# Scoring two attention heads together in the row halves of TensorE, with a new order of the work around it

## What is computed

```python
q, k = rms_norm(q, q_gain), rms_norm(k, k_gain)
logits = q @ k.T / 8 + bias[head, key] + mask[query, key]
p = softmax(logits)
o = p @ v
y = rms_norm(o by group of heads) * (a gate, for the forgetting heads)
x = x + y @ w_out
```

## Time and profile before

| | |
|---|---|
| median of 3 runs | 1564.51 us |
| the profiled execution | 1565.74 us, span 1563.9 us |
| PE matmul busy | 1496.9 us, 96% of the span |
| DVE busy, ACT busy | 844.1 us (54%), 616.3 us (39%) |
| granted TensorE clock, mean | 0.986 |
| chain that ended last | PE 85%, DVE 7%, POOL 4%, ACT 2% |
| the attention stage, in the trace | about 924 to 1180 us |

### The profile page before, as it was taken

One profiled execution on the slowest core, in us unless ns is written; L12 is line 12 of the kernel. 1 busy time (PEld: TensorE's weight loads), 2 busy tenths in 40 slices (PEclk: granted clock), 3 DMA queues, 4 the chain that ended last, 5 costly groups with the idle time before them and its releaser, 6 DMA issues.

```text
span 1563.9 us, 23462 instructions
## 1 busy us (share of the span) xinstructions
PE 1496.9 (96%) x9229; PEld 1290.1 (82%) x9229; DVE 844.1 (54%) x1227; ACT 616.3 (39%) x920; POOL 267.0 (17%) x272
## 2 busy tenths in 40 slices
PE   7978999999979999999997999999999999999998
PEld 7977999999968988988885777888886888888887
DVE  5779744357465543553455546776845533434344
ACT  5547655643243221231233334646534323223230
POOL 2664100000025613540632000000100000000000
PEclk9989999999999999999998999999999999999999
DMA  5211211123302222222232221111122222223221
GB/s 191 83 42 54 69 54 56 67 82 137 108 28 95 94 94 94 91 97 95 81 108 74 73 76 55 43 39 55 41 81 95 91 97 95 95 94 95 92 95 67
DMA packets 36006, 128.03 MB, mean 82 GB/s; under 512 B 4460, under 2 KB 4588, under 8 KB 35792
## 3 DMA queue, kind: packets, MB, share of 16 engines
q1 hardware_dynamic: 34464, 122.18, 23.3%
q10 hardware_dynamic: 864, 4.33, 0.7%
q0 software_dynamic: 592, 0.30, 0.1%
HBM read 124.68 MB, written 2.10 MB: 81 GB/s over the span
## 4 chain that ended last, share of the span: by engine, by line
PE 85%; DVE 7%; POOL 4%; ACT 2%; issue 2%; DMA 0%; SPq 0%; DVEq 0%; POOLq 0%; ACTq 0%
PE ps L1699 72%; PE ps L2036 2%; PE ps L2060 2%; PE ps L1881 1%; PE ps L1723 1%; POOL phase_tmp L1568 1%; PE ps L2047 1%; PE ps L1831 1%; DVE h_lo L866 1%; DVE w_lo L853 1%; PE ps L2014 1%; DVE x L866 1%; POOL acc L1568 1%; POOL phase L1568 1%; POOL conv_tmp L1657 1%
## 5 line engine op out<-in xcount | busy, mean ns | idle before, releaser
L1699 PE MATMUL ps<-h_hi,w_hi 128*128 128x258 f32 (+2 forms) x1768 | 512.3, 339 | 38.9 <-DVE h_lo L866 18.2
L1699 PE MATMUL ps<-h_lo,w_hi 128*128 128x258 f32 (+2 forms) x1768 | 494.3, 329 | 0.0
L1699 PE MATMUL ps<-h_hi,w_lo 128*128 128x258 f32 (+2 forms) x1768 | 493.2, 328 | 0.0
L853 DVE TENSOR_TENSOR w_lo<-w_raw,w_hi 128x1024 fp32r<-128x1024 f32 (+2 forms) x227 | 290.5, 1280 | 182.6 <-ACT w_hi L355 181.4
L1699 PEld LDWEIGHTS ps<-h_hi,w_hi 128*128 128x128 f32 x1768 | 301.9, 190 | 90.1 <-issue 34.8
L1699 PEld LDWEIGHTS ps<-h_lo,w_hi 128*128 128x128 f32 x1768 | 299.5, 190 | 33.8 <-issue 5.9
L1699 PEld LDWEIGHTS ps<-h_hi,w_lo 128*128 128x128 f32 x1768 | 299.5, 190 | 30.8
L355 ACT ACTIVATE w_hi<-w_raw 128x1024 fp32r<-128x1024 f32 (+2 forms) x227 | 233.2, 1035 | 199.6 <-PE ps L1699 198.6
L1699 PE MATMUL ps<-mlp_lo,w_hi 128*128 128x512 f32 x256 | 100.9, 394 | 0.0
L1699 PE MATMUL ps<-mlp_hi,w_hi 128*128 128x512 f32 x256 | 100.3, 392 | 0.0
L1699 PE MATMUL ps<-mlp_hi,w_lo 128*128 128x512 f32 x256 | 99.4, 388 | 0.0
(11 more groups left out here) (292 smaller groups left out, 1936.3 us busy)
## 6 DMA issues: line engine op xcount, KB each, us to landing
w_raw<-w_units SPq DMA_DIRECT2D x227, 512.0 KB, 3.3
x<-x_t ACTq DMA_DIRECT2D x1, 2112.0 KB, 7.8
out<-out_tile SPq DMA_DIRECT2D x8, 256.0 KB, 2.0
x<-x_t ACTq DMA_DIRECT2D x3, 528.0 KB, 9.2
x<-x_t ACTq DMA_DIRECT2D x2, 264.0 KB, 4.7
consts<-consts SPq DMA_DIRECT2D x1, 320.0 KB, 6.9
b_step<-ssm_b SPq DMA_DIRECT2D x1, 256.0 KB, 10.4
c_step<-ssm_c SPq DMA_DIRECT2D x1, 256.0 KB, 11.3
```

The costliest lines, as they stand in the source:

```text
L853: Dv.do(v.tensor_tensor(wlo[:, s % RING, 0:w], raw[:, s % RING, 0:w], f32(whi[:, s % RING, 0:w]), ALU.subtract), lo_ready)
L1699: ins = mm(o, wt[:, s % RING, w], xt[:, kx, c0:c0 + n], start=(b == 0 and a == 0), stop=(b == len(blocks) - 1 and a == 2))
```

## The change

1. Scores. q and k of a pair are kept as 128 rows (tiles q_pair, k_pair: head 0 in rows 0 to 63, head 1 in rows 64 to 127). One call scores both heads: first all masks of the pair, then for query tiles 1 and 3 the bias and the product of q and k, then the same for tiles 0 and 2. Bias and product of the two heads go to the two row halves of the array (`tile_position=(64 * hh, 0)`), each to its own PSUM bank. The bias is an fp32r matmul of its own: a selector (pair_sel_r) picks the head's row of key_bias_r, in which rows 0 to 15 hold the rounded bias and rows 32 to 47 the rest of it. The semaphore qk_mm is raised after each half.
2. Set-up. One DMA of 256 KB brings all linear biases, four small ones the forgetting heads' rows; 16 DMAs in the loop go away, and so do the two memsets of the ones (L1314). ACT gains two copies (pair_sel_r, key_bias_r), DVE two subtractions of 16x512, POOL three additions on 8 columns.
3. `qk_norm` ends in one operation of 128 rows for both heads, where it had two of 64 rows.
4. `maxima` and `exps` go by the query tiles 1, 3, 0, 2, and start on tile 1 when the first half of the scores is there.
5. Order. On PE both heads' transposes stand together after wide(i,1), and both heads' values after wide(i+1,0), followed by stat and the scores of the pair. On ACT a one-element exponential ahead of `exps` loads its table; both heads' exponentials follow each other. The tail is ordered in the same manner, and out_part(5) and (6) leave PSUM (DVE) after the dilated group's norm, where they stood before it.

```diff
-BANK_DONE = (3, 2, 3, 4)
+BANK_DONE = (4, 1, 4, 2)
+    T_ORDER = (1, 3, 0, 2)
...
             def maxima(i, hh):
-                dve.wait_ge(sem("qk_mm"), h + 1)
...
-                for t in range(4):
+                for t in T_ORDER:
+                    if t in (T_ORDER[0], T_ORDER[2]):
+                        dve.wait_ge(sem("qk_mm"), 2 * i + 1 + T_ORDER.index(t) // 2)
...
-            def scores(i, hh):
-                pe.wait_ge(sem("aug_ready"), 4 * i + 4)
-                pe.wait_ge(sem("qa_ones"), 2)
-                pe.wait_ge(sem(f"bias_in{i % 2}"), 32 * (i // 2 + 1))
-                if i:
-                    pe.wait_ge(sem("attn_done"), h - 1)
...
+            def scores(i):
+                pe.wait_ge(sem("aug_ready"), 2 * i + 2)
+                pe.wait_ge(sem("bias_lo"), 2)
...
+                rows_of = (slice(0, 64), slice(64, 128))
+                for t in T_ORDER:
...
+                    if t == 0 and i:
+                        pe.wait_ge(sem("attn_done"), 2 * i)
+                    for hh in range(2):
+                        if 2 * i + hh < N_MOBA + N_FOX:
+                            mm(PS[:, 2 + 3 * hh + bank, c + w - P:c + w], identr[:, :], maskr[:, :], start=(t != 2), stop=True,
...
+                for ts in (T_ORDER[:2], T_ORDER[2:]):
+                    for t in ts:
...
+                        for hh in range(2):
+                            mm(PS[:, 2 + 3 * hh + bank, c:c + w], selr[rows_of[hh], i, :], kbr[rows_of[hh], 0:w],
+                               start=False, stop=True, skip_group_check=True, tile_position=(64 * hh, 0))
+                    for t in ts:
...
+                        for hh in range(2):
+                            r = rows_of[hh]
+                            ins = mm(PS[:, 2 + 3 * hh + bank, c:c + w], qa[i % 2][r, P * t:P * t + P], ka[i % 2][r, 0:w],
+                                     start=False, stop=True, skip_group_check=True, tile_position=(64 * hh, 0))
+                    ins.then_inc(sem("qk_mm"), 1)
```

PE's loop:

```diff
                 if i >= 2:
-                    p_transposes(i - 2, 1)
+                    values(i - 2, 0)
...
                 qk_stat(i, 0)
+                scores(i - 1)
...
                 p_transposes(i - 1, 0)
-                scores(i - 1, 1)
-                values(i - 1, 0)
+                p_transposes(i - 1, 1)
                 qk_stat(i, 1)
```

PE's tail:

```diff
             out_part(0)
+            values(KT - 2, 0)
+            values(KT - 2, 1)
...
             out_part(1)
-            p_transposes(KT - 2, 1)
-            scores(KT - 1, 0)
-            values(KT - 2, 1)
+            scores(KT - 1)
             out_part(2)
             out_part(3)
             p_transposes(KT - 1, 0)
-            scores(KT - 1, 1)
+            p_transposes(KT - 1, 1)
+            out_part(4)
             values(KT - 1, 0)
-            out_part(4)
+            values(KT - 1, 1)
             out_part(5)
```

ACT's loop:

```diff
+                A.do(dn.activation(small[:, 481:482], small[:, 490:491], ACT.Exp))
+                exps(i - 1, 0)
+                exps(i - 1, 1)
                 qk_rsqrt(i, 0)
...
+                split_hi(qk_unit(i, 1) + LOOK)
                 qk_square(i, 1)
```

DVE's loop:

```diff
+                maxima(i - 1, 0)
                 if last:
                     fox_gate(3)
...
+                maxima(i - 1, 1)
+                qk_ms(i, 0)
+                split_lo(qk_unit(i, 1) + LOOK)
...
                 qk_evac(i, 1)
```

More of the change, by code:

```diff
@@ L766, in _ @@
                     group_rsqrt(2, 0, 2)
-                if not last:
-                    split_hi(qk_unit(i, 1) + LOOK)
+                split_hi(qk_unit(i, 1) + LOOK)
                 qk_square(i, 1)
[L770 to L781, removed]
+            for m in range(4):
+                y_hi(m)
+            pt_copy(KT - 2, 0)
+            y_hi(4)
+            qk_rsqrt(KT - 1, 1)
+            pt_copy(KT - 2, 1)
             split_hi(U_OA + 2)
             split_hi(U_OA + 3)
-            pt_copy(KT - 2, 1)
+            A.do(dn.activation(small[:, 481:482], small[:, 490:491], ACT.Exp))
             exps(KT - 1, 0)
+            exps(KT - 1, 1)
             split_hi(U_OA + 4)
@@ L1420, in _ @@
                 last = i == KT - 1
+                if i >= 2:
+                    qk_ms(i - 1, 1)
+                    pt_copy(i - 2, 0)
+                    pt_copy(i - 2, 1)
+                    qk_norm(i - 1, 1)
                 qk_evac(i, 0)
+                split_lo(qk_unit(i, 0) + LOOK)
                 if i >= 2:
-                    pt_copy(i - 2, 1)
-                maxima(i - 1, 0)
+                    attn_out(i - 2, 0)
                 if last:
@@ L1428, in _ @@
                     attn_out(i - 2, 1)
+                maxima(i - 1, 0)
                 if last:
                     fox_gate(3)
[L1431 to L1432 removed]
                 if i == KT - 2:
                     group_ms(0, 2)
[L1435 to L1441 removed]
+                maxima(i - 1, 1)
+                qk_ms(i, 0)
+                split_lo(qk_unit(i, 1) + LOOK)
                 if i == KT - 2:
                     group_norm(1, 0, 2)
[L1444 to L1459 removed]
+                qk_evac(i, 1)
+                if not last:
+                    qk_norm(i, 0)
+            fox_gate(4)
+            for m in range(4):
+                y_lo(m)
+            qk_ms(KT - 1, 1)
+            y_lo(4)
+            pt_copy(KT - 2, 0)
+            pt_copy(KT - 2, 1)
+            qk_norm(KT - 1, 0)
+            qk_norm(KT - 1, 1)
             split_lo(U_OA + 2)
@@ L1464, in _ @@
             split_lo(U_OA + 3)
[L1465 removed]
+            attn_out(KT - 2, 0)
+            attn_out(KT - 2, 1)
             out_part(1)
             maxima(KT - 1, 0)
[L1468 removed]
+            maxima(KT - 1, 1)
             split_lo(U_OA + 4)
@@ L2103, in _ @@
                 if i >= 2:
-                    p_transposes(i - 2, 1)
+                    values(i - 2, 0)
                 if last:
                     group_tile(1)
-                scores(i - 1, 0)
-                if last:
-                    group_tile(2)
                 if i >= 2:
@@ L2112, in _ @@
                 if last:
+                    group_tile(2)
+                if last:
                     group_tile(3)
                 qk_stat(i, 0)
+                scores(i - 1)
                 pe.wait_ge(sem("qms_ready"), 2 * i)
```

124 lines of the change are left out of this document (49 added, 75 removed).

## The result

| | before | changed |
|---|---|---|
| median | 1564.58 us (8 runs, beside the changed kernel) | 1572.51 us (8 runs, 1567.6 to 1572.9) |
| profiled execution | 1565.74 us, span 1563.9 | 1572.46 us, span 1570.7 |
| PE matmul busy | 1496.9 us, 96% | 1492.5 us, 95% |
| mean granted clock | 0.986 | 0.983 |

The account below looks back on a forecast made before the run. PE bounds the attention stage (busy 204.90 of 205 us). PE's work -10.3, waits +19.1 and startup -1.4 sum to +7.4, taken as +6.5: median 1571.0 us, forecast's own range 1567.6 to 1577, overall 1561.0 to 1583.0.

Parts of the forecast that it names:

- PE's work: Scoring on PE: row halves fully overlapped, less bias and switches, save 1.28 us a pair, -10.3 us in eight.
- The 1.54: Alternative speedup of two row tiles in the q-k product, from the skill page: 2.9 us for 2.2, sum -4.7.
- The wait of rounds 1 to 5: PE waits ahead of stat(i,1) for the chain over ACT and DVE: 1.9 us a round, 9.5 in all.
- The other waits: New PE waits in rounds 1, 6, 7 and the tail: 1.7, 2.7, 1.3, 1.6, 2.5, 0.9 us; one of 1.1 goes.
- out_part(0): PE waits there for y_lo(4), ready at 13.4 us against PE's 10.9: 2.5 us.
- The clock: Granted clock in the attention stage: up to one fall counted within the forecast, each costing 1.7 us.
- (c): Rival: clock falls in the stage's new waits, 1575 with two or three falls, up to 1584; chance 0.17.
- The dummy exponential helps nobody here: On ACT ahead of exps: already idle 1.94 us until the maxima, so a table load fits in it.
- Startup: Ahead of the stage: memsets leave DVE, PE's 1.24 us wait for the gate's copy goes, -1.4 us.
- (a): Rival: chain ahead of stat hidden, five waits of rounds 1 to 5 gone, faster, 1558.6 us; chance 0.14.
- (d): Rival: row halves don't overlap in scoring, 2.8 us more a pair, +22, 1594 us; chance 0.05.
- (b): Rival: about even, each new wait half of the sum, -2 us, 1562.3; chance 0.14.

Follow-up runs that it names:

- group_first: copy_first with the group norm's three small steps of round 6 moved ahead of w_lo on DVE: 1558.39 us, ratio 0.9966 to the kernel before.
- copy_first: Changed kernel with DVE's copy qk_raw of the second projection moved ahead of w_lo and round 6's group norm steps: 1566.9 us median, in two bands.
- no_dummy: Changed kernel without its eight dummy exponentials, which load ACT's table early: 1580.35 us, ratio 1.0101 to the kernel before.
- all_no_dummy: Changed kernel reordered to remove every nameable wait (1545.48 us), then without its dummy exponentials: 1549.8 us, ratio 0.9905 to the kernel before.
- heads_apart: Changed kernel with bias and q-k products issued head by head within each half of the tiles, not in turn: 1573.97 us, ratio 1.0054 to the kernel before.

## Why the prediction was right, and where it was not

**Sign, size and place: right.** PE's work for a pair falls, and the new order of DVE gives more back in waits. group_first shows it: with the same scores and only the copy and three small steps moved on DVE, the kernel is faster than before. That the size came out within 2 us is in part luck, as the clock below shows.

**PE's work: right.** Forecast 1.28 us less for a pair. The round without a wait is 24.76 - 23.53 = 1.23 less. By parts, in the round shown: the bias 1.14 with the switch into the row halves (0.63 + 0.2 taken), the product 1.85 (2.2 taken), the switch back 0.1 (0.2 taken; the unit behind the scores takes 5.68 where 24 matmuls at 0.23 are 5.58). The masks' row starts at 1035.61, but stat's two matmuls end at 1036.17, their stream 0.16 ahead of that, at 1036.01: from there to the bias at 1036.94 the eight masks take 0.93 (0.87 taken). In all 4.0 where I forecast 4.1. The overlap is 1.93 times of 2. The 1.54 that I worked out from the page "TensorE: Matmul & The Clock Gate" of the Trainium skill would have been too dear; that page measures four row tiles, and this kernel's two lose little (2.99 us where half of 5.77 would be 2.89).

**The wait of rounds 1 to 5: right.** Forecast 1.9 in each. The row says 1.60, and the round is 25.39 - 23.53 = 1.86 longer than without. Idle time in a row is counted from the recorded end of the last matmul, 0.16 behind the end of its stream, and the weights are waited for again; I had counted from the stream. The chain came out as summed, each link within 0.1 us, and 0.2 shorter in all.

**The other waits: their sum was too high.** Measured 1.45 (1.7 forecast), 2.37 (2.7), 0.97 (1.3), 1.57 (1.6), 0.40 (0.9), and the 1.1 us ahead of the last values went. The failing term is out_part(0): forecast 2.5, measured nothing (the row at 1135.20 has no idle). I let it wait for the fifth y_lo; but `unit` waits block by block, the first matmuls need y_lo(0) alone, and the others come while it works (DVE ends the fifth at 1138.06, the fifth block's first matmul starts at 1138.29). With 0.27 a wait for stream and weights (1.86 less 1.60) the new waits come to 5 x 1.86 + 6.76 + 5 x 0.27 = 17.4 and the one that went to 1.4: 16.0, against 19.1 forecast.

**The clock: more than I counted, less than (c).** One new fall behind the 2.37, worth 1.7 us, and 1.4 more in the tail; forecast was up to one. The two misses, 3 us too many in waits and 3 too few in clock, cancel, which is luck: -9.8 (eight times 1.23, as an estimate) + 16.0 + 3.1 - 1.5 = 7.8, measured 7.4. The rule of the page "TensorE: Matmul & The Clock Gate" of the Trainium skill, that transposes don't count as busy for the gate, did not come true as I had worked it out ("nearly every wait here would bring a fall"): between 952 and 1102.7 six waits, five of them behind twenty transposes, left the clock at 1.00:

```profile
952.00:1102.70 150.70, 138.99 (x830) 111.57 (x828) 90.92 (x162) 83.05 (x178) 1.30 (x3) 1.00 0.13 44
```

In copy_first and without the dummies such waits were followed by falls, and not always. In no_dummy four rounds have the same wait of 2.66 us; behind three of them the clock fell, behind the one at 1054.29 it didn't (the second row; the first is the one at 1026.39):

```profile
1026.20:1029.50 3.30, 3.10 (x6) 1.84 (x6) 3.20 (x6) 1.21 (x3) 0.00 (x0) 0.51 0.42 154
1054.20:1057.60 3.40, 3.31 (x13) 2.38 (x14) 3.30 (x7) 1.31 (x3) 0.00 (x0) 1.00 0.35 136
```

The wait of 3.2 us in the tail was followed by 6.7 us at half clock in the changed kernel, 3.4 in group_first and none in no_dummy. So the length of a wait alone doesn't decide; what does stays open.

**"The dummy exponential helps nobody here": wrong.** no_dummy costs 7.8 us, all_no_dummy 4.3. I had seen that ACT was idle long enough to hide a load, and not asked when the load is issued: the row at 1015.25 shows it behind the wait of the instruction that needs it. The forecast was not touched, since the dummies were in the kernel; the reason was.

**Startup: right.** 1.4 forecast, 1.5 measured in the trace and alone.

**Rivals.** (a) was one swap away: 1558.6 forecast for a hidden chain, 1558.39 measured in group_first. That they agree so closely is chance: group_first has four waits of 0.35 us ahead of the masks that (a) doesn't know. (d)'s price is confirmed, its case is out. (b) needed half the waits.

## What to carry to other kernels

When an engine's time is one long chain of ordered work, ask of each wait which instruction behind it could already run. Here a copy stood behind a w_lo that waited for something unrelated, and its place, with that of the group norm's steps, was worth some 11 us, about as much as the arithmetic saved on TensorE (eight times 1.23); a gain in work shows only once the waits that it uncovers are moved away. And where an engine waits for data ahead of an instruction that needs another table, try an early table load: here it was worth 7.8 and 4.3 us. Last, before a difference of 2 us between two kernels is explained, the clock of their executions has to be compared: here one fall more or less is 1.7 us, and it came and went without any edit.

## What the runs showed of the hardware that I had not expected

- Matmuls on different row halves start out of the order in which they were issued (heads_apart, 1038.90), so that two heads' products in separate runs of matmuls cost only 0.46 us more than in turn. "TensorE: Matmul & The Clock Gate" of the Trainium skill, in its part on packing, speaks of a reorder window for weight loads, which fits, and says that matmuls themselves start strictly in order, which these rows contradict.
- A table load without its own early trigger is not started in the idle time ahead of its instruction: ACT was idle for 6.28 us and loaded then (1015.25).
- A short wait can cost several times itself: 1.48 us ahead of 1099.45 were followed by 13.6 us at the clock of 1.2 GHz in one order, and in seven of twelve executions the time was some 9 us longer. With the wait at 0.20 us it was so in none of six. Longer waits (2.66 us at 1054.29, 3.18 in no_dummy's tail) left the clock at 2.4 GHz in other executions, so the wait makes a fall possible and not certain.
